# One block's mixing stage rearranged: attention heads staggered over steps, compression products turned round, gating ahead of its use

## The reference, cut to what matters

```
h = rms_norm(x, norm_mix)
z_a, z_b, z_cq, z_ckv_c, z_ckv_s, z_ckv_w, z_cg = split(h @ w_in)
out_a = spatial_gating(z_a, ...)        # gelu, layer norm of v, 4 groups of 128x128, u * (w v + b)
out_b = dilated_attention(q, k, v)      # 4 heads of 128, 256 x 256 scores with a bias
out_c = nsa_attention(q_c, ...)         # 8 heads; keys and values compressed, plain, windowed; gates
    # compress_blocks: 2 groups x 15 blocks of 32 tokens + pos -> gelu(blocks @ w1) @ w2, for k and v
x = x + concat(out_a, out_b, out_c) @ w_out
h = rms_norm(x, norm_xattn); q = h @ xattn_wq; kv = rms_norm(mem) @ xattn_wkv
x = x + softmax(q k^T) v @ xattn_wo     # 4 heads of 128, 256 x 256 scores
x = x + square(relu(rms_norm(x) @ w_up)) @ w_down
```

## Time and profile before

| what | value |
|---|---|
| median of three runs | 3080.54 us |
| the profiled execution's own time | 3080.89 us |
| its span in the trace | 3079.4 us |
| mean granted clock of TensorE | 0.988 |
| TensorE matmul busy | 2993.7 us (97%) |
| VectorE busy | 2178.0 us (71%) |
| ScalarE busy | 1461.0 us (47%) |
| DMA | 648.60 MB, mean 211 GB/s |

### The profile page before, as it was taken

The page is one execution under the profiler, slowest core; times in us unless marked ns, Lnnn a source line. Parts: engine busy times, 40 slices in busy tenths (PEclk is TensorE's granted clock), DMA queues, the critical chain, the costliest instruction groups (busy, mean ns, idle before and its releaser), DMA issues.

```text
span 3079.4 us, 40253 instructions
## 1 busy us (share of the span) xinstructions
PE 2993.7 (97%) x16588; PEld 2553.5 (83%) x16588; DVE 2178.0 (71%) x2686; ACT 1461.0 (47%) x1953; POOL 8.5 (0%) x21
## 2 busy tenths in 40 slices
PE   8999998999999999999999999999999999999998
PEld 7877787888888888877787778888878888888886
DVE  6455766799889986778766666648888775555557
ACT  5434555544444444545454443544546444444444
POOL 0000000000000000000000000000000000000000
PEclk9989899999999999999999999999999999999999
DMA  6544233577677786556754445558656765555553
GB/s 257 189 153 182 95 137 137 198 262 264 250 259 263 280 314 219 191 213 232 262 218 161 176 170 184 218 219 327 228 182 225 282 245 186 184 191 183 186 192 110
DMA packets 106661, 648.60 MB, mean 211 GB/s; under 512 B 11856, under 2 KB 11856, under 8 KB 42352
## 3 DMA queue, kind: packets, MB, share of 16 engines
q1 hardware_dynamic: 99936, 621.86, 55.0%
q10 hardware_dynamic: 4608, 16.78, 1.4%
q0 software_dynamic: 1936, 7.41, 0.7%
HBM read 635.52 MB, written 10.49 MB: 210 GB/s over the span
## 4 chain that ended last, share of the span: by engine, by line
PE 85%; DVE 10%; ACT 3%; issue 2%; DMA 1%; SPq 0%; ACTq 0%; DVEq 0%
PE PS L496 46%; PE PS L497 23%; DVE RL L1963 3%; PE PS L534 3%; PE PS L536 3%; PE PS L535 3%; DVE G L2374 1%; ACT RH L1169 1%; PE PS L734 1%; PE PS L1024 1%; PE PS L936 1%; ACT G L1376 1%; PE PS L870 0%; PE PS L916 0%; DMA RW<-in_w_ckv 0%
## 5 line engine op out<-in xcount | busy, mean ns | idle before, releaser
L496 PE MATMUL PS<-A,RH 128*128 128x512 f32 x4544 | 1629.5, 403 | 28.5 <-DVE RL L1963 11.2
L1963 DVE TENSOR_TENSOR RL<-RW,RH 128x1024 fp32r<-128x1024 f32 x974 | 1178.4, 1222 | 559.3 <-ACT RH L1169 553.0
L1169 ACT ACTIVATE RH<-RW 128x1024 fp32r<-128x1024 f32 x974 | 1015.9, 1054 | 780.9 <-PE PS L497 634.9
L497 PE MATMUL PS<-A,RL 128*128 128x256 f32 x4544 | 1279.4, 282 | 0.0
L496 PEld LDWEIGHTS PS<-A,RH 128*128 128x128 f32 x4544 | 861.7, 190 | 245.5 <-issue 31.6
L497 PEld LDWEIGHTS PS<-A,RL 128*128 128x128 f32 x4544 | 865.6, 190 | 3.1 <-issue 2.6
L496 PE MATMUL PS<-H,RH 128*128 128x512 f32 x2304 | 814.0, 395 | 1.3 <-DVE RL L1963 1.3
L497 PE MATMUL PS<-H,RL 128*128 128x256 f32 x2304 | 651.4, 283 | 0.0
L496 PEld LDWEIGHTS PS<-H,RH 128*128 128x128 f32 x2304 | 432.8, 188 | 101.3 <-issue 1.2
L497 PEld LDWEIGHTS PS<-H,RL 128*128 128x128 f32 x2304 | 433.2, 188 | 0.4
L1176 ACT ACTIVATE LT<-PS 128x512 f32<-128x512 f32 x232 | 138.3, 596 | 346.3 <-PE PS L497 345.9
(11 more groups left out here) (253 smaller groups left out, 1598.3 us busy)
## 6 DMA issues: line engine op xcount, KB each, us to landing
RW<-in_w_fin SPq DMA_DIRECT2D x88, 1024.0 KB, 4.8
G<-in_w_ada SPq DMA_DIRECT2D x160, 512.0 KB, 5.9
RW<-in_w_up SPq DMA_DIRECT2D x64, 1024.0 KB, 4.9
RW<-in_w_down SPq DMA_DIRECT2D x64, 1024.0 KB, 5.0
RW<-in_w_fout SPq DMA_DIRECT2D x44, 1024.0 KB, 4.8
RW<-in_w_v SPq DMA_DIRECT2D x32, 1024.0 KB, 4.8
RW<-in_w_bg SPq DMA_DIRECT2D x32, 1024.0 KB, 4.9
RW<-in_w_k SPq DMA_DIRECT2D x16, 1024.0 KB, 4.8
```

The lines of the kernel that those rows point to most:

```text
L496: t.matmul(bank[:, :], wh[:, k, cols], x, start=first and k == 0, stop=False, skip_group_check=True)
L497: done = t.matmul(bank[:, 0:256], wl[:, k, cols], x[:, 0, :], start=False, stop=last and k == 3, skip_group_check=True)
L1169: a.activation(m.high(x), m.slot(j)[:, x % 2 * HC:x % 2 * HC + HC], ACT.Copy).then_inc(s["hi"], 1)
L1963: v.tensor_tensor(m.low(x), m.slot(j)[:, x % 2 * HC:x % 2 * HC + HC], m.high(x).bitcast(F32), ALU.subtract).then_inc(s["lo"], 1)
```

## The change

It does seven things. (1) Compression: the blocks are now the stationary operand (30 columns) and the weights the moving one (128 columns), so the hidden layer comes out turned; ScalarE applies gelu to it, TensorE turns it back, ScalarE copies it, and the second layer follows. B1 becomes two buffers, written for k and v at the start, with the blocks of one product side by side. The four chunks come in four steps one after another. (2) Gating runs beside compression, both token halves together, one hop between ScalarE and VectorE at each step; its products come in the eighth step. (3) The dilated heads are staggered: in step k the scores of head k, the exponentials and probabilities of head k - 1, the transposes of head k - 2 and the value product of head k - 3. (4) The gates' sigmoid and transposes run beside vsw. (5) `mixed_ab` runs beside vsw too, each piece when vsw has used the part of AH that it overwrites. (6) `cross` is staggered in the same way. (7) `feeding(2)` waits for each part of X by itself and for the last product of xo.

```diff
-        self.B1 = self.VSW[:, 0:960]
+        self.B1 = self.KSW[:, 0:960], self.VSW[:, 0:960]
+        self.hid = [self.bufs[3 + i][0:30, 0:128] for i in range(2)]
...
# TensorE
+    def gates_turned():
+        yield
         bk = banks.next()
         wait_empty(bk)
         t.wait_ge(s["gate_a"], 1)
         t.transpose(bk.ap[:, 0:32], m.GT[0:32, 0:128], ident[0:32, 0:32])
         t.transpose(bk.ap[:, 32:64], m.GT[0:32, 128:256], ident[0:32, 0:32]).then_inc(bk.full, 1)
+        yield
+        yield
...
     def compress():
+        def chunk(which, c):
...
+                done = t.matmul(hid[which].ap[0:30, 0:128], m.B1[which][:, 30 * jj:30 * jj + 30],
+                                w[:, i * 128:i * 128 + 128], start=jj == 0, stop=jj == 31)
+        def turn(which):
+            bk = banks.next()
+            wait_empty(bk)
+            t.wait_ge(hid[which].empty, hid[which].n)
+            t.transpose(bk.ap[:, 0:30], m.hid[which], ident[0:30, 0:30]).then_inc(bk.full, 1)
+            return bk
+        chunk(0, 0)
+        yield
+        chunk(0, 1)
+        yield
+        chunk(1, 0)
+        yield
+        chunk(1, 1)
+        first = turn(0)
+        yield
+        yield
+        second(0, first)
+        first = turn(1)
+        yield
+        yield
+        second(1, first)
+        yield
+        yield
     def gmlp():
-        yield
+        yield from idle(7)
         bk = [banks.next(), banks.next()]
+        t.wait_ge(s["gm_v"], 10)
         for i in range(2):
-            t.wait_ge(s["gm_v"], 1 + 5 * (i + 1))
...
     def dilated():
+        for k in range(7):
+            if 2 <= k < 6:
+                tr[k - 2] = turned(unit[k - 2])
+            if k >= 3:
+                attend([(tr[h], lambda k, h=h: m.VB[...], 128)])
+            if k < 4:
+                unit[k] = scores(m.QKB[...], m.QKB[...])
+            yield
...
# ScalarE
     def gmlp():
+        sm, W = m.sms[0], m.bufs[0:2]
         evacuated(num.va)
+        for i in range(2):
+            a.activation(W[i], m.VA[...], ACT.Copy, accum_out=sm[:, i:i + 1]).then_inc(s["gm_a"], 1)
+        yield
+        yield
+        for i in range(2):
+            a.wait_ge(s["gm_v"], 4 + i)
+            a.activation(W[i], m.VA[...], ACT.Square, accum_out=sm[:, 2 + i:3 + i]).then_inc(s["gm_a"], 1)
+        yield
+        yield
+        yield
         a.preload_act_table_set("natural_log_exp_and_others")
+        a.wait_ge(s["gm_v"], 6)
+        a.activation(sm[:, 4:6], sm[:, 2:4], ACT.Ln).then_inc(s["gm_a"], 1)
+        a.wait_ge(s["gm_a"], 5)
+        a.activation(sm[:, 6:8], sm[:, 4:6], ACT.Exp, scale=-0.5).then_inc(s["gm_a"], 1)
+        yield
         yield
     def mixed_ab():
+        n = num.half
+        yield
         a.wait_ge(s["gw"], 2)
+        a.wait_ge(whole[3].empty, whole[3].n)
         for i in range(4):
+            a.wait_ge(s["used"], n + i + 1)
             a.activation(m.AH[...], src, ACT.Copy).then_inc(s["xh"], 1)
+            yield
+        yield from idle(3)
     # cross: in step k
+            if 2 <= k < 6:
+                tr[k - 2] = turned_end(turn, causal=False)
+            if k < 4:
+                exponentials(unit, direct=True)
+            if k >= 3:
+                attend_end(out, m.AH[...], True)
     # feeding
-                if use == 2 and p == 0:
-                    evacuated(num.block - 1)
+                if use == 2:
+                    if p == 0:
+                        a.wait_ge(s["used"], num.half)
+                    evacuated(num.xo + p)
...
# VectorE, gating, seventh step
+        v.wait_ge(s["gm_a"], 6)
+        for i in range(2):
+            v.scalar_tensor_tensor(va[i], va[i], sm[:, 6 + i:7 + i], m.ca("ln_g"), ...).then_inc(s["gm_v"], 1)
+        for i in range(2):
+            v.wait_ge(s["gm_v"], 7 + i)
+            v.tensor_tensor(va[i], va[i], m.ca("ln_b"), ALU.add).then_inc(s["gm_v"], 1)
     # dilated: in step k
+            if k < 4:
+                unit[k] = scores_max(m.ca("dil"))
+            if 1 <= k < 5:
+                at[k - 1] = probabilities(unit[k - 1])
...
# SyncE
     def compress():
+        for k in range(4):
+            send(PLAIN[k] + NW)
+            num.plain += 1
+            yield
+        yield from idle(5)
...
# the schedule
-    run(chain(L.compress(), L.gmlp(), L.dilated()), chain(L.w_in("qc"), L.w_in("ksw"), L.gates(), L.w_in("vsw")))
-    L.mixed_ab()
+    run(chain(both(L.compress(), L.gmlp()), L.dilated()), chain(L.w_in("qc"), L.w_in("ksw")))
+    L.gates()
+    run(L.mixed_ab(), L.gates_turned(), L.w_in("vsw"))
```

More of the change, by code:

```diff
@@ L740, in dilated @@
         evacuated(num.rows["vb"])
[L741 to L751, removed]
+        unit, tr = {}, {}
+        for k in range(7):
+            if 2 <= k < 6:
+                tr[k - 2] = turned(unit[k - 2])
+            if k >= 3:
+                h = k - 3
+                attend([(tr[h], lambda k, h=h: m.VB[:, k * 512 + h * 128:k * 512 + h * 128 + 128], 128)])
+            if k < 4:
+                unit[k] = scores(m.QKB[:, k * 256:k * 256 + 256], m.QKB[:, 1024 + k * 256:1280 + k * 256])
+            yield
     L.compress, L.gmlp, L.dilated = compress, gmlp, dilated
-    L.mixed_ab = lambda: None
+    L.mixed_ab = lambda: idle(8)
     def nsa():
@@ L823, in cross @@
         evacuated(num.rows["xv"])
[L824 to L834, removed]
+        unit, tr = {}, {}
+        for k in range(7):
+            if k < 4:
+                unit[k] = scores(m.XQ[:, k * 256:k * 256 + 256], m.XK[:, k * 256:k * 256 + 256])
+            if 2 <= k < 6:
+                tr[k - 2] = turned(unit[k - 2], causal=False)
+            if k >= 3:
+                h = k - 3
+                attend([(tr[h], lambda k, h=h: m.XV[:, k * 512 + h * 128:k * 512 + h * 128 + 128], 128)])
+            yield
     L.cross = cross
@@ L1378, in scores, with turned_begin, turned_end @@
         x.then_inc(done, 1)
-    def turned(n=256, causal=True):
-        bk = banks.next()
+    def scores(n=256):
+        exponentials(scores_begin(), n)
+    def turned_begin():
+        return banks.next()
+    def turned_end(bk, n=256, causal=True):
         at = att["pt0"] + att["pt"] % att["npt"]
@@ L2210, in scores @@
         return at
+    def scores(bias, gate=None, valid=None, n=256):
+        return probabilities(scores_max(bias, n), gate, valid, n)
     def turned(at):
@@ L2328, in cross @@
         scr_free.clear()
[L2329 to L2337 removed]
+        unit, at = {}, {}
+        for k in range(7):
+            if k < 4:
+                unit[k] = scores_max(None)
+            if 2 <= k < 6:
+                turned(at[k - 2])
+            if 1 <= k < 5:
+                at[k - 1] = probabilities(unit[k - 1])
+            if k >= 3:
+                d = slice((k - 3) * S, (k - 2) * S)
                 attend(m.AL[:, d], m.AH[:, d])
[L2339 to L2340 removed]
+            yield
     L.cross = cross
@@ L3072, in gates @@
         small()
-        return
-        yield
     def compress():
-        for which in range(2):
-            for c in range(2):
-                send(PLAIN[2 * which + c] + NW)
-                num.plain += 1
-                yield
+        for k in range(4):
+            send(PLAIN[k] + NW)
+            num.plain += 1
             yield
+        yield from idle(5)
     L.gates, L.compress = gates, compress
-    L.gmlp = L.dilated = L.nsa = L.cross = idle
-    L.mixed_ab = L.fed_rest = nothing
+    L.nsa = idle
+    L.gmlp, L.dilated = lambda: idle(10), lambda: idle(7)
+    L.cross = lambda: idle(7)
+    L.gates_turned = lambda: idle(3)
+    L.mixed_ab = lambda: idle(8)
+    L.fed_rest = nothing
     L.memory = lambda: idle(9)
```

294 lines of the change are left out of this document (161 added, 133 removed).

## The result

The changed kernel takes 3049.24 us (median of four runs, 3044.88 to 3051.58). The kernel before takes 3079.35 us over all its runs here. The ratio is 0.9898, with a 95% interval of 0.9885 to 0.9911: faster by 1.0%.

The account below looks back on a forecast made before the run. TensorE was taken to bound the kernel, but not in the changed stretch, with its waits and low clock. Gains of 10.1 (mixing), 0.9 (next stage), 8.8 (cross) and 0.65 (feeding), together 20.4 us, gave 3060 us, range 3052 to 3069.

Parts of the forecast that it names:

- Sigmoid and mixture: In mixing: TensorE's waits for the sigmoid (1.9 us) and the rounded mixture (2.4 us) go, now covered by vsw.
- Dilated heads: In mixing: four waits of 5.6 us go, with a 1.6 us clock loss; new waits cost 0.6 us, bounds 0 and 4.
- First half of qc: In mixing: two ScalarE Copies with a sum now precede its rounding, so TensorE's 0.22 us wait grows by 1.5 us.
- Gating's new wait: In mixing: a 12.8 us chain through qc's late fifth chunk makes TensorE wait 3.5 us, bounds 2.0 and 5.0.
- Feeding: After cross: the first scaling no longer waits for the last addition to X; gain 0.65 us, bounds 0.4 and 1.5.
- Next stage: After mixing: VectorE starts its heads free and reaches the first full scores earlier; gain 0.9 us, bounds 0 and 6.
- Chunks: Compression in mixing: the new shape adds 0.5 us for 128 records, and turning the hidden layer 0.2 us.
- rival in which the pace follows the stationary columns: Compression chunks: loads alone set the pace, so the pitch falls to half, 7.3 us less, 3052 us; chance 0.03.
- slower rival: Mixing, steps 1 to 7: long f32 runs hold the clock at 1.2 GHz, +35 us, 3095 us; chance 0.05.
- Gating's clock: In mixing: 16 f32 gating records behind the new wait run at 1.2 GHz, costing 3.8 us, between 2.5 and 5.0.
- Cross: First scores to xo: 14.1 us, including 1.5 us for low clock, against 22.9; gain 8.8 us, bounds 5 and 10.3.
- the first rival: More goes: the next stage's first wait shrinks, its clock stays up; about 7 us more likely, 3053 us; chance 0.11.

Follow-up runs that it names:

- thirty_moving: The changed kernel with only the compression chunks' orientation undone (weights stationary, 30 block columns moving, no turning): 3056.97 us, ratio 0.9926.

## Why the prediction was wrong in size

**What held.** The direction, the mechanism of every part and nearly every wait.
- Sigmoid and mixture: 1.9 and 2.4 us gone, both seen again in the kernel that takes the cover away.
- Dilated heads: 5.6 us gone; 4.8 us of waits come back with the old order.
- First half of qc: 1.47 us; grows by 1.25, forecast 1.5.
- Gating's new wait: 3.18 us against 3.5, its chain 12.5 us against 12.8 (the parts as the forecast lists them add up to 12.9).
- Feeding: 0.7 us against 0.65. Next stage: 0.83 us against 0.9, its first wait 3.5 us instead of 4.6. That the total fits so well is in part luck, because this stage lost 10.2 us to the clock in both first profiles, but 5.1 in the second profile before and 6.8 in the second and third after.
- Chunks: the forecast's 0.7 us came, about 0.35 us by four chunks and 0.35 by two turnings. The pitches it compared were not of one kind: 0.114 counts the modelled end of the last record, 0.11 and 0.150 go from start to start. From start to start the chunk had 0.109 us before and has 0.110 now. The rival in which the pace follows the stationary columns is refuted.
- The slower rival, the turned compression at 1.2 GHz, did not show either: mixing has clock 1.00.

**What failed.** The prediction took the clock's losses as fixed, and sized them wrongly in three of five terms. The figures are those of the profiled execution, where 32.6 us went against 20.4:
- *Gating's clock*, "The cost is between 2.5 and 5.0; I take 3.8". It was 0 in the first profile. Over the seven profiles with turned chunks and a gating wait of 3.0 to 3.2 us the loss is 0, 1.7, 3.4, 3.4, 1.7, 0 and 1.7 us, a mean of 1.7. What it cost is less: mixing took 126.35, 127.90 and 129.0 us in the changed kernel's three profiles, with 0, 1.7 and 3.4 us lost. I had sized the term from windows where the clock did fall, and excluded the case where it doesn't. This is the step that failed most: 3.8 us here, at least 2.1 on average.
- *Cross*, "I add 1.5 us" for 1.2 GHz, and the 12.6 us below it. The clock stayed at 1.00 in all of the stage. That is 1.5 us, and the chain itself was 0.7 us shorter than I placed it: 11.94 us. Together 2.2.
- *Behind cross* I counted 0.65 us and left the clock out. In the first profile before, xo's products ran partly at 0.50, and 2.2 us more went than forecast. The second profile before lost only 0.4 us there and took 26.5 us from xo to up, and the old order of cross 26.5 as well, against 25.9 and 25.5 after. So this term rests on one execution.
- *Small costs of mixing*: the dilated 0.6 us did not come, the gating wait and the first half of qc were 0.3 and 0.25 us less. Together 1.1 us, each within its bounds, all on one side. Another 0.5 us of mixing fits no single term; the windows credited as going held 7.3 us of lost clock, and 8.5 had been lost.
- *Outside the change*: 3.0 us beyond 540 us, where the instructions are the same, less 0.6 us at the start, where the profiles here scatter from 149.5 to 151.5 us. Behind 614 us all profiles scatter against each other by up to 5.4 us, so the 3.0 us are not put down to the change.

3.8 + 2.2 + 2.2 + 1.1 + 0.5 + 3.0 - 0.6 is 12.2, the difference. Against the medians the miss is 10.8 us. The second profiles of both kernels divide a difference of 34.1 us otherwise: 15.9 in mixing, 11.9 in cross, 0.7 from xo to up, 7.1 beyond it, and -1.5 in the rest. Mixing and cross hold in both, the terms behind them don't.

**Where the gain comes from.** Up to 620 us the clock lost 27.3 us in the first profile before and 11.9 in the first after, so of 32.6 us up to 15.4 are clock. The forecast had a net 6.8: in mixing 1.6, 3.2 and 2.5 against 3.8, and in cross the old 22.9 x 0.21 = 4.8 against 1.5. Measured it is 8.5 in mixing, where nothing was lost after, 4.8 in cross and about 2 behind it. The next stage lost 10.2 us in both.

**The range.** Its lower end was the end of the rivals, 3052. It came from a forecast that charged 3.8 and 1.5 us of clock as certain. With nothing for these the forecast is 3054.7, and the first rival, which takes about 7 us more, would have carried the range to about 3048. The clock in xo's products stood in no case at all.

**What stays open.** What decides in an execution whether the clock falls behind a given wait. The runs show only that it is not the wait's length alone: 3.18 us left it up and 3.1 us did not, in the same kernel; 2.51 us left it up where 2.24 us did not, and inside chunks of 30 moving columns it fell with no wait in front. No run tried to steer it.

## What to carry to other kernels

List the places where the clock may fall, and give each a chance and not a certainty: here 0 to 3.4 us of clock were lost behind a wait of about 3 us, 1.7 on average. The second profile of the unchanged kernel is enough to see it. When a change empties a stage of its waits, allow for the clock of the work behind that stage too, which was 0.4 to 2.2 us here. And when a chain ends in a late load, count what stands between the load and the waiter on every in-order engine: it decides better than the number of steps how far to move the waiter, and one step too far brings the wait back.

## What the runs showed of the hardware

- The clock can fall without idle time of TensorE in front. With 128 stationary and 30 moving columns it fell inside the first and the second chunk of `thirty_moving` (0.56 and 0.60 over the windows at 153.8 and 164.0 us). With 30 stationary and 128 moving columns it fell at the chunks in none of ten profiles.
- The columns of the stationary operand didn't set the pace of these f32 products: 3.61 us for 32 records with 30 of them, 3.48 to 3.52 us with 128, from the first record to the start of the next group.
- The same program loses other stretches in each execution. Up to 620 us, before: 27.3 us in both profiles, at different places. After: 11.9, 8.5 and 13.7 us in three.
- The load of the ScalarE table at gating took 1.28 us, and the next instruction began 0.02 us behind it, in every profile here.
